# Expert matrices loaded as 2 MB pairs, raw memory transposes, two more tiles beside the ring, values by head pair

## The reference, cut to what matters

```python
x += sum_i sigmoid(h @ w_gate_i) * (branch_i(h) @ w_branch_i) @ w_out   # h = rms(x) * g; i = A, B, C
m = _rms_norm(mem, mem_norm_g)                   # keys and values of the cross attention
k, v = (m @ w_xkv) split;  x += softmax(q @ k / 8) @ v @ w_xo
# experts: top group of 4, then the top 2 of its 8 experts; 32 experts in all
y_e = (silu(xb @ w1[e]) * (xb @ w3[e])) @ w2[e]  # w1, w3: 1024 x 512, w2: 512 x 1024; 2 MB each
x += sum over chosen e of gate_e * y_e
```

## Time and profile before

| | us |
|---|---|
| median of 3 runs | 1718.87 |
| lowest, highest | 1715.06, 1721.05 |
| the profiled execution's own time | 1717.54 |
| its span (first to last instruction) | 1715.4 |
| mean granted TensorE clock | 0.905 |

### The profile page before, as it was taken

The page is one execution under the profiler, slowest core; times in us unless marked ns, Lnnn a source line. Parts: engine busy times, 40 slices in busy tenths (PEclk is TensorE's granted clock), DMA queues, the critical chain, the costliest instruction groups (busy, mean ns, idle before and its releaser), DMA issues.

```text
span 1715.4 us, 18172 instructions
## 1 busy us (share of the span) xinstructions
PE 1375.3 (80%) x7588; PEld 824.1 (48%) x7588; DVE 531.1 (31%) x1042; ACT 231.5 (13%) x552; POOL 35.0 (2%) x45
## 2 busy tenths in 40 slices
PE   5999999998666556777689999999986665676665
PEld 5887688854222123232258776887542121322211
DVE  5134646435111311221121345643432211212122
ACT  2013330022000000000011144100310000000000
POOL 2000000001000000000000000000000000000000
PEclk9999999999887878798889999999998787888888
DMA  9843227445999999999995332454489999999995
GB/s 310 270 140 99 74 70 246 157 178 217 408 421 421 422 420 421 421 421 421 421 348 171 111 111 69 118 215 168 172 324 421 421 422 421 418 421 421 422 422 234
DMA packets 137925, 505.57 MB, mean 295 GB/s; under 512 B 8688, under 2 KB 80176, under 8 KB 88432
## 3 DMA queue, kind: packets, MB, share of 16 engines
q1 hardware_dynamic: 134288, 492.98, 73.8%
q0 software_dynamic: 2704, 8.22, 1.5%
q10 hardware_dynamic: 848, 3.15, 0.5%
HBM read 503.27 MB, written 1.05 MB: 294 GB/s over the span
## 4 chain that ended last, share of the span: by engine, by line
PE 55%; DMA 39%; DVE 2%; SPq 2%; issue 1%; ACT 1%; POOL 0%; DVEq 0%; ACTq 0%; POOLq 0%
DMA ring<-in_w_dram 37%; PE banks L1435 26%; PE banks L1622 6%; PE banks L1662 5%; PE banks L1441 4%; PE banks L1734 3%; SPq L487 2%; PE banks L1546 1%; PE banks L1556 1%; PE banks L1582 1%; DMA k<-in_w_xkv_dram 1%; PE banks L1542 1%; PE banks L1591 1%; PE banks L1720 1%; PE banks L1487 0%
## 5 line engine op out<-in xcount | busy, mean ns | idle before, releaser
L1622 PE MATMUL banks<-ring,v 128*32 128x512 f32 x1936 | 302.9, 771 | 188.7 <-DMA ring<-in_w_dram 180.9
L1435 PE MATMUL banks<-hT,ring 128*128 128x256 f32 (+1 forms) x1472 | 327.6, 383 | 1.9 <-ACT hT L617 1.9
L1435 PEld LDWEIGHTS banks<-hT,ring 128*128 128x128 f32 (+1 forms) x1472 | 277.5, 190 | 48.4 <-issue 5.0
L1622 PEld LDWEIGHTS banks<-ring,v 128*32 128x32 f32 x1936 | 81.8, 136 | 397.1 <-issue 393.0
L1662 PE MATMUL banks<-ring,probT 128*32 128x512 f32 x1024 | 154.5, 730 | 88.3 <-DMA ring<-in_w_dram 80.0
L1662 PEld LDWEIGHTS banks<-ring,probT 128*32 128x32 f32 x1024 | 40.8, 131 | 190.4 <-issue 179.9
L1171 DVE COPY q<-banks 128x512 f32<-128x512 f32 x16 | 11.1, 692 | 246.6 <-PE banks L1662 246.6
L1591 PE MATMUL banks<-v,h 128*128 128x128 f32 x512 | 68.5, 297 | 13.3 <-issue 11.9
L1591 PEld LDWEIGHTS banks<-v,h 128*128 128x128 f32 x512 | 65.0, 209 | 27.2 <-issue 27.2
L1167 DVE TENSOR_TENSOR prob<-banks,prob 128x512 f32<-128x512 f32 x16 | 11.1, 692 | 205.6 <-PE banks L1622 205.6
L1160 DVE TENSOR_SCALAR prob<-prob 128x512 f32<-128x512 f32 x16 | 6.8, 427 | 184.8 <-ACT prob L698 184.8
(11 more groups left out here) (261 smaller groups left out, 1282.2 us busy)
## 6 DMA issues: line engine op xcount, KB each, us to landing
ring<-in_w_dram SPq DMA_DIRECT2D x370, 1024.0 KB, 19.1
ring<-in_w_in_dram SPq DMA_DIRECT2D x52, 1024.0 KB, 11.9
ring<-in_w_branch_dram SPq DMA_DIRECT2D x8, 1024.0 KB, 5.1
ring<-in_w_out_dram SPq DMA_DIRECT2D x8, 1024.0 KB, 5.9
k<-in_w_xkv_dram POOLq DMA_DIRECT2D x4, 1024.0 KB, 17.8
ring<-in_w_branch_dram SPq DMA_DIRECT2D x8, 512.0 KB, 3.5
k<-in_w_dram SPq DMA_DIRECT2D x4, 1024.0 KB, 8.6
shared<-in_w_dram SPq DMA_DIRECT2D x4, 1024.0 KB, 6.3
```

The lines of the kernel that those rows point to most:

```text
L1435: last = nc.tensor.matmul(dst, w[:, k, cols], src[:, k, :], start=k == 0, stop=k == kn - 1)
L1622: last = nc.tensor.matmul(bank[2 + m][e * CAP:(e + 1) * CAP, :], xt[:, k, e * CAP:(e + 1) * CAP], ws[e][:, r * D_EXPERT:(r + 1) * D_EXPERT ...
```

## The change

- Groups 1 to 6: one expert's matrix comes as one 2 MB load with runs of 16 KB into a pair of neighbouring slots (`pair_source`, `quad_pairs`). SP waits until both slots are free; PE waits for the landing of the pair. The two parts of the work are now the two halves of each pair, and the slots are freed 8 at a time, behind part 1. Groups 0 and 7 keep tiles of 1 MB, with rows taken in the new order (`RUN_IN`, `RUN_OUT`).
- Two tiles of group 0's w2 come ahead beside the ring, in `prob` + half of `probT`, and in `gain` + `oa` (`EXTRA` 9, `AHEAD`, `load_beside`). The routing's scratch tiles move to `q1` and `v1`; the loads of gains on the POOL queue are moved to later.
- The memory rows are transposed raw; the norm's gain is applied per row of the transposed copy (`mcol`), the root on the keys (`mem_rstd`, spread by two matmuls of a diagonal with ones) and on the values.
- Start: SP first loads the identity and layer 0's memory weights, tables after the third turn; three small matmuls (`stay_warm`) stand around the memory transposes; the memory values are made behind `turn_tokens`, the tables set up behind them.
- Attention: `products(u)` once for each head pair with 256 query columns; the transposed probabilities of a pair lie in `probT` or `gain` by turns.

The diff, cut to its core:

```diff
-EXTRA = 7
+EXTRA = 9
+AHEAD = [KD + i for i in range(7)] + [2 * KD, 2 * KD + 1]
...
+        def in_pairs(q):
+            return 0 < q < QUADS - 1
...
         def quad_at(q, j):
-            return Q_BASE + j + (EXTRA if q == 0 and j < KD else 0)
+            if in_pairs(q):
+                w, (part, e) = j // KD, divmod(j % KD, QUAD)
+                return Q_BASE + w * KD + 2 * e + part
+            return Q_BASE + j + (sum(a > j for a in AHEAD) if q == 0 else 0)
...
+        def pair_source(l, q, w, e):
+            w, run = ((w1, RUN_IN), (w3, RUN_IN), (w2, RUN_OUT))[w]
+            return w[l][bass.ds(q * QUAD + e, 1), :, :].rearrange("e (p r) n -> p e (r n)", r=run)
...
+                def quad_pairs(q):
+                    for w in range(3):
+                        for e in range(QUAD):
+                            at = quad_at(q, w * KD + e)
+                            sp.wait_ge(slot_free, l * PER_LAYER + q * PER_QUAD + (at + 2))
+                            s = at % RING
+                            both = ring[:, s:s + 2, :].rearrange("p a n -> p (a n)").rearrange("p (k n) -> p k n", k=1)
+                            sp.dma_start(both, pair_source(l, q, w, e)).then_inc(landed[s], 16)
...
# SP at the start
+            sp.dma_start(con[:, 0:C_SWAP], consts[:, 0:C_SWAP]).then_inc(id_in, 16)
+            sp.dma_start(wxk, w_xkv[0, :, 0:256]...).then_inc(first_wxk_in, 16)
+            sp.dma_start(wxv, w_xkv[0, :, 256:512]...).then_inc(first_wxv_in, 16)
+                    if j == 3 and l == 0:
+                        load_tables()
...
# PE, experts_round
+                        if q is not None and in_pairs(q):
+                            in_ring = KD * part
                         if in_ring:
                             last.then_inc(free, in_ring)
...
-                        last.then_inc(free, n)
+                        if q is None or not in_pairs(q):
+                            last.then_inc(free, n - sum(beside_ring(2 * KD + part * QUAD + e) for e in range(first, first + n)))
+                        elif part == 1:
+                            last.then_inc(free, KD)
...
                     def wait_main(j):
-                        at = quad_at(q, j)
+                        at = quad_at(q, j) - in_pairs(q) * (quad_at(q, j) % 2)
...
# PE, the start
+            stay_warm(1, bank[2], C_SWAP)
+            mem_turn(0, 1)
+            stay_warm(2, bank[2], C_SWAP)
             mem_turn_copied(0)
             mem_keys(0)
-            mem_values(0)
             for l in range(DEPTH):
                 turn_tokens(l)
+                if l == 0:
+                    mem_values(0)
...
-                    if i >= LAG_PV:
-                        products(l, i - LAG_PV)
+                    if i >= LAG_PV and (i - LAG_PV) % 2 == 1:
+                        products(l, (i - LAG_PV) // 2)
```

More of the change, by code:

```diff
@@ L163 @@
 A0, B0, C0, X0, NI = 0, 8, 16, 24, 28
+PRODUCED = X0 // 2 + NI - X0
 OUTS = 14
@@ L334, in bass_hybrid_encoder, with signals @@
         more_free = sem("more_free")
+        def in_pairs(q):
+            return 0 < q < QUADS - 1
+        def signals(j):
+            if j < len(TURNS):
+                return TURNS[j][0] != "empty"
+            return not (in_pairs((j - Q_BASE) // PER_QUAD) and j % 2)
         def real_turns(slot, upto):
-            return sum(1 for j in range(upto) if j % RING == slot and
-                       (j >= len(TURNS) or TURNS[j][0] != "empty"))
+            return sum(1 for j in range(upto) if j % RING == slot and signals(j))
         def wait_turn(eng, l, j):
@@ L371, in slot_flat, with beside @@
             return ring[:, j % RING, :]
-        def beside(i):
-            return extras[i].rearrange("p (k n) -> p k n", k=1)
+        def beside(i, c):
+            at = 512 * c
+            for part in extras[i]:
+                if at < part.shape[1]:
+                    return part[:, at:at + 512]
+                at -= part.shape[1]
         def plain(eng):
@@ L405, in turned_n, with unit_probsT @@
             return bank[b][:, (at + k % 2) * P:(at + k % 2 + 1) * P]
+        def unit_probsT(u):
+            both = gain[:, :] if u % 2 else probT[:, :, :, :, :].rearrange("p b j c n -> p (b j c n)")
+            return both.rearrange("p (j c n) -> p j c n", j=2, c=TT)
         def score_banks(i):
@@ L480, in _, with quad_turns @@
                 sp.wait_ge(mix_sum, l * 4 + 3)
-                sp.dma_start(beside(1), quad_source(l, 0, KD + 1)).then_inc(extra_in[1], 16)
-                def quad_turns(q, first, last=PER_QUAD):
-                    for j in range(first, last):
+                load_beside(l, 1)
+                def quad_turns(q, turns):
+                    for j in turns:
                         at = quad_at(q, j)
@@ L715, in _ @@
             act.wait_ge(eps_set, 1)
+            nc.scalar.activation(small[:, 63:64], stat[:, 8:9], ACT.Square)
             mem_squares(0)
@@ L1595, in gather, with experts_round, beside_ring, weights @@
                         last.then_inc(S["gathered"], 1)
-            def experts_round(S, wait, free, rd, look, extras_in=None, gather_rest=None, at_w3=None, at_look=None, last_group=QUAD):
+            def experts_round(S, wait, free, rd, look, extras_in=None, q=None, gather_rest=None, at_w3=None, at_look=None, last_group=QUAD):
                 xts = rd + 1
+                def beside_ring(j):
+                    return extras_in is not None and j in AHEAD
+                def weights(j):
+                    if beside_ring(j):
+                        i = AHEAD.index(j)
+                        pe.wait_ge(extra_in[i], extras_in * len(extras[i]))
+                        return lambda c: beside(i, c)
+                    wait(j)
+                    w = slot_flat(j if q is None else quad_at(q, j))
+                    return lambda c: w[:, c * 512:(c + 1) * 512]
                 pe.wait_ge(S["xt_act"], xts)
@@ L1654, in experts_round @@
                     for first in range(0, QUAD, n):
-                        for e in range(first, first + n):
-                            wait(2 * KD + part * QUAD + e)
+                        ws = {e: weights(2 * KD + part * QUAD + e) for e in range(first, first + n)}
                         for half in range(2):
```

421 lines of the change are left out of this document (248 added, 173 removed).

## The result

The changed kernel took 1777.14 us (median; 1775.66 to 1779.50), the kernel before on the same chip 1719.96: a ratio of 1.0336 (95% interval 1.0314 to 1.0358), slower. Forecast were 1742 us, 1702 to 1762. The direction was right, the size was not: the loss is 57 us where 23 were forecast, and the time lies outside the range. The profiled execution spans 1773.4 us at a mean granted clock of 0.877.

What follows compares the result with a forecast made beforehand. The prediction took memory at 421 GB/s to bound the experts and PE most of the rest. It summed 1717.5 + 35.2 (experts) - 7.4 (start) - 2.9 (values) = 1742.4, said 1742 us, range 1702 to 1762.

Steps and rivals of the forecast that it cites:

- The pace of the experts, and how it would turn: Experts stages: now at memory's pace, 421 GB/s; after the change PE and the queue wait for each other at each matrix.
- every sign that it named: Experts: rate about 400, DMA dips after landings, x64 blocks every 21.4 us, chain from free through a load of about 12 us.
- Freeing in eights: Experts, groups 1 to 6: the free comes after 11.04 us against 9.24 us queued; 17 stalls of 1.8 us, 30.6 us a layer.
- What the stalls were to absorb: Layer 0's experts: memory loads for layer 1 pass partly in stalls (-3.0 us), memory keys keep PE warm (-1.8 us).
- Runs of 16 KB: Expert loads: a pair takes 4.90 us against two tiles of 2.49; 0.33 us for each of 36 matrices, 11.8 us.
- Two tiles ahead: Group 0's w2: two tiles loaded before the experts begin leave the flat stretch, 5.0 us less in each layer.
- no stall at full clock: Experts: a matrix takes PE 7.1 us, so the free comes at 8.9 us, before 9.24; 1687 us, 12% chance.
- The start: Kernel start: first projection at 31.4 us against 38.9, -7.4 us (ends -3.5 and -10).
- The hazard that the text named: Start: 1 KB rows of the keys' weights alternate badly with 4 KB rows of other queues, land at 17 us; gain only -3.5.
- Values by head pair: Attention products of B and C: a pair takes 1.0 us instead of 1.18; 16 pairs, -2.9 us (ends -4.8, +1.3).
- This counts in full: Attention: PE is never idle long there, so the -2.9 us of the products shortens the whole time.
- the stall's own upper end of 3.0 us: Experts: first part 6.4 us, second 3.64, 2.0 lost give a 3.0 us stall per matrix; 1783 us, above 1760 4%.

Runs made afterwards that it cites:

- E11: The changed kernel with most expert matmuls of groups 1 to 6 left out, all loads, waits and frees kept; 1695.9 us.
- E12: E9 (runs of 8 KB) with most expert matmuls of groups 1 to 6 left out; 1700.1 us.
- E4: The changed kernel with groups 1 to 6 back on 1 MB tiles freed in fours, and seven tiles ahead beside the ring instead of nine; 1714.0 us.
- E5: The changed kernel with idle matmuls (15, 9, 9) filling PE's waits up to the landing, to keep its clock high; 1749.7 us.
- E10: E3 with x loaded on SP's queue behind the memory keys' weights; 1700.7 us.
- E6: E3 with each head pair's products done in two halves of 128 query columns; 1707.8 us.
- E14: E9 with the idle matmuls of E5 put in; 1781.2 us.
- E3: The changed kernel with each 2 MB load holding the same part of two experts (8 KB runs), slots freed in fours; 1702.6 us.
- E9: E3 with slots freed in eights at the end of the matrix and PE waiting for all four loads before its first matmul; 1772.6 us.
- E2: The changed kernel with fewer idle matmuls (12, 9, 4) in PE's waits in groups 1 to 6; 1781.7 us.

## Why the prediction was right in kind and wrong in size

- **The pace of the experts, and how it would turn.** Right, with every sign that it named: x64 blocks, a dip after each landing, a chain of load and matrix by turns.
- **Freeing in eights: stall of 1.8 us per matrix.** This is the step that failed, and by size alone: the stall measured 2.5 us (22.21 less 19.72). PE's part was forecast at 9.2 and is 9.3. The other part, free to next matrix, was 0.05 + 1.65 + 9.80 + 0.56 + 0.14 = 12.2 and is 12.9 on the mean (12.7 as median). The term that was mis-sized is the data left in the queue at a landing. It was forecast at 9.24 us, as if all of both open loads but the last 0.56 us were still to come. It measured 3.63 MB (mean of the same 15), 8.6 us at 421 GB/s. The marks give the gap: the last comes 0.61 us behind their mean, so by the landing the other parts of the queue are that far into the next loads, and 9.24 less 0.61 is 8.6. So 0.14 + 9.3 + 0.05 - 8.6 = 0.9 us are lost before the free, where the forecast had 0.15. The restart was right: the rates of the three microseconds behind the free are 8, 262 and 274 GB/s on the mean, which loses 1.7 us (forecast 1.65). 0.7 us too little, 34 times (layer 1's stall taken for both layers), is 24 of the 30 us that the experts are over the forecast.
- **What the stalls were to absorb.** The memory's loads for layer 1 were booked at -3.0, the memory keys at -1.8. Layer 0 lost 33.7 us, layer 1 31.8: nothing was absorbed.
- **Runs of 16 KB: -11.8 us.** 0.23 us a matrix, 36 times, would be -8 by layer 1, and layer 0 shows no gain; the medians of E11 and E12 say -4. The estimate from the Trainium skill (DMA: Bandwidth & Descriptors, "Why small descriptors are slow") was -4: the medians agree with it, and layer 1 alone lies between it and the -11.8.
- **Two tiles ahead: -10.0 us.** Measured by E4 at 10.0 between medians.
- **The rival "no stall at full clock", 1687 us.** It rested on 8.9 < 9.24. E5 ran mostly at full clock and kept a stall (21.2 us a matrix; 3.16 MB, 7.5 us, to move behind a landing); only E11, with most of PE's work gone, had none, at 1696.
- **The start: -7.4 us.** -4.6 at the first projection (34.3 us where it was 38.9). The hazard that the text named came true: beside 4 KB packets the 1 KB packets of the keys' weights passed at 39 to 59 a microsecond (7 to 13 us), against 300 and more alone. E10 shows it as the cause of the late weights.
- **Values by head pair: -2.9 us.** PE's busy time fell by 2.6 us in a layer; the stage didn't get shorter (E6). "This counts in full" was wrong.
- **The sum.** With what was measured it closes: 1717.5 + 65.4 (experts) - 6.2 (their start in layer 0) - 1.4 (the stretch between) = 1775.3, where the forecast had 1717.5 + 35.2 - 7.4 - 2.9. The range was too narrow above: the stall's own upper end of 3.0 us gave 1783, and the text left 4% to all above 1760.

## What to carry to other kernels

A ring that is freed late is safe as long as what is left in the queue at a landing outlasts the work up to the free and the restart. Of the 4.19 MB that were open on paper, 3.6 MB were left in the changed kernel and 2.9 in E14, so count on two thirds of the open loads, not on all. A stall that repeats 34 times multiplies the error of its estimate by 34: its upper end belongs in the range. Longer runs were worth some 1% of a matrix's time at best and 0.2% of the whole here, and an order of loads that lets PE start and free in parts (E3) keeps both the large load and the full rate.

## What the runs showed of the hardware that was not expected

- A load of 2 MB lands in sixteen parts that don't end together: 0.9 us apart where the queue had just run dry (changed kernel, E9), 2.8 us where it never did (E3), up to 3.6 us in E14. 6 to 7.3 us after a landing the rate fell, where 9.9 us of data were open.
- Queues take turns by packet, not by bytes. From 8 to 12 us the changed kernel moved 192 packets on SP's queue and 188 each on ACT's and POOL's:

```profile
q10 hardware_dynamic: 188, 0.74, 53.0%
q0 software_dynamic: 188, 0.49, 36.1%
q1 hardware_dynamic: 192, 0.20, 14.2%
```

- Keeping PE warm across a load is no sure gain: 27 us less in E5, nothing in E2 and 9 us more in E14 than without it, with a mean granted clock of 0.94 to 0.97 in all three.
